# Second MLP in pairs of column chunks, with seven block products in 32 of its units

## The reference

```python
h2 = _rms_norm(x, norm2_g[l])
x = x + (jax.nn.silu(h2 @ w_gate[l]) * (h2 @ w_up[l])) @ w_down[l]
```

## Time and profile before

| | |
|---|---|
| median of 3 runs | 2490.76 us (2490.45 to 2491.49) |
| the profiled execution's own time | 2491.81 us |
| its span | 2490.1 us |
| PE busy | 2479.4 us in 11851 matmuls |
| DVE, ACT, POOL busy | 1379.7, 1120.4, 116.4 us |
| moved by DMA | 467.11 MB, mean 188 GB/s |

### The profile page before, as it was taken

The page is one execution under the profiler, slowest core; times in us unless marked ns, Lnnn a source line. Parts: engine busy times, 40 slices in busy tenths (PEclk is TensorE's granted clock), DMA queues, the critical chain, the costliest instruction groups (busy, mean ns, idle before and its releaser), DMA issues.

```text
span 2490.1 us, 27992 instructions
## 1 busy us (share of the span) xinstructions
PE 2479.4 (100%) x11851; PEld 2073.6 (83%) x11851; DVE 1379.7 (55%) x1130; ACT 1120.4 (45%) x1100; POOL 116.4 (5%) x95
## 2 busy tenths in 40 slices
PE   9999999999999999999999999999999999999999
PEld 7888888888888888888888888788888888888887
DVE  5775455454655555545555568876544444444444
ACT  5545533334444434334434458874533333333332
POOL 0410010010100000000000010000200000000000
PEclk9999999999999999999999999999999999999999
DMA  7555465656656555555555555444555655565554
GB/s 250 174 181 185 154 202 186 202 187 199 223 189 204 194 191 186 197 191 186 195 191 188 186 186 186 138 160 160 186 186 186 198 191 186 187 200 187 187 190 147
DMA packets 243306, 467.11 MB, mean 188 GB/s; under 512 B 11312, under 2 KB 23104, under 8 KB 242798
## 3 DMA queue, kind: packets, MB, share of 16 engines
q1 hardware_dynamic: 241630, 460.08, 56.8%
q10 hardware_dynamic: 1552, 5.25, 0.6%
HBM read 463.20 MB, written 2.10 MB: 187 GB/s over the span
## 4 chain that ended last, share of the span: by engine, by line
PE 97%; DVE 1%; ACT 1%; issue 0%; DMA 0%; POOL 0%; SPq 0%; DVEq 0%; ACTq 0%; POOLq 0%
PE acc L423 26%; PE acc L414 26%; PE acc L416 26%; PE acc L443 5%; PE acc L449 2%; PE tp L443 2%; PE sd L443 2%; PE sd L449 1%; PE tp L449 1%; PE tp L469 1%; PE sd L1377 1%; PE tp L1395 0%; DVE wlo L399 0%; PE sd L1386 0%; ACT whi L391 0%
## 5 line engine op out<-in xcount | busy, mean ns | idle before, releaser
L399 DVE TENSOR_TENSOR wlo<-raw,whi 128x2048 fp32r<-128x2048 f32 (+1 forms) x440 | 1014.0, 2306 | 955.7 <-ACT whi L391 955.0
L391 ACT ACTIVATE whi<-raw 128x2048 fp32r<-128x2048 f32 (+1 forms) x440 | 832.3, 1893 | 1068.7 <-PE acc L423 920.3
L414 PE MATMUL acc<-whi,opA_hi 128*128 128x512 f32 x1888 | 741.1, 393 | 0.0
L416 PE MATMUL acc<-whi,opA_lo 128*128 128x512 f32 x1888 | 735.4, 390 | 0.0
L423 PE MATMUL acc<-wlo,opA_hi 128*128 128x512 f32 x1888 | 469.2, 390 | 0.2 <-DVE wlo L399 0.2
L414 PE MATMUL acc<-whi,opB 128*128 128x512 f32 (+1 forms) x1088 | 422.3, 389 | 1.5 <-ACT whi L391 1.5
L416 PE MATMUL acc<-whi,opB 128*128 128x512 f32 (+1 forms) x1088 | 419.0, 386 | 0.0
L414 PEld LDWEIGHTS acc<-whi,opA_hi 128*128 128x128 f32 x1888 | 354.8, 188 | 73.9 <-issue 0.9
L416 PEld LDWEIGHTS acc<-whi,opA_lo 128*128 128x128 f32 x1888 | 354.8, 188 | 72.6
L423 PEld LDWEIGHTS acc<-wlo,opA_hi 128*128 128x128 f32 x1888 | 353.0, 188 | 73.4 <-DVE wlo L399 0.8
L423 PE MATMUL acc<-wlo,opB 128*128 128x512 f32 (+1 forms) x1088 | 266.4, 387 | 0.1
(11 more groups left out here) (307 smaller groups left out, 1286.8 us busy)
## 6 DMA issues: line engine op xcount, KB each, us to landing
raw<-in_w_in SPq DMA_DIRECT2D x114, 1024.0 KB, 5.5
raw<-in_w_mlp_up SPq DMA_DIRECT2D x64, 1024.0 KB, 5.5
raw<-in_w_mlp_down SPq DMA_DIRECT2D x64, 1024.0 KB, 5.0
raw<-in_w_gate SPq DMA_DIRECT2D x44, 1024.0 KB, 5.1
raw<-in_w_up SPq DMA_DIRECT2D x44, 1024.0 KB, 5.2
raw<-in_w_down SPq DMA_DIRECT2D x44, 1024.0 KB, 5.0
raw<-in_w_out SPq DMA_DIRECT2D x32, 1024.0 KB, 5.0
raw<-in_w_branch SPq DMA_DIRECT2D x16, 1024.0 KB, 5.0
```

The source lines that it names most:

```text
L391: eng.activation(whi[:, j % SPL, k, 0:cols], raw[:, j, k, 0:cols], ACT.Copy).then_inc(hi_split, share(k))
L399: eng.tensor_tensor(wlo[:, j % SPL, k, 0:cols], raw[:, j, k, 0:cols], whi[:, j % SPL, k, 0:cols].bitcast(F32), ALU.subtract).then_inc(lo_s ...
L414: eng.matmul(acc[:, pair, m, 0:cols], hi[:, kt + i, m * P:(m + 1) * P], whi[:, s, i, 0:cols], start=first and i == 0, stop=False)
L416: eng.matmul(acc[:, pair, m, 0:cols], lo[:, kt + i, m * P:(m + 1) * P], whi[:, s, i, 0:cols], start=False, stop=False)
```

## The change

A **pair** takes two runs in one: for a chunk c a gate pair does gate and up together, and a down pair does two neighbouring 512-column chunks of the output. A unit is now 2 k-tiles by 2 chunks (b = 0, 1), loaded by two DMAs of 512 KB, and all four banks `acc[:, b, m]` are in use by each pair. 17 pairs: in the parts of 3, 4 and 4 chunks, gate pairs of 8 units and two down pairs of 6, 8 and 8.

A plain unit has the same 24 matmuls. In a pair's first and last unit they go bank by bank (6 each, high then low), since the four banks are emptied and freed one by one (bank_done, bank_read, silu_in).

A **seven-unit** multiplies its 2 x 2 blocks of activations (m by k-tile) and 2 x 2 blocks of weights (k-tile by b) with seven products of sums in place of eight (Strassen's scheme in Winograd's form): 21 matmuls. Gate pairs have them at v = 3 and 5 (the first at 5 alone), down pairs at 3 and 5 (in part 0: the first at 3, the second at 1 and 3). It needs
- sums of the weight blocks: GpSimd, `weight_sums`, three instructions into t_sum, one buffer;
- seven blocks split high and low: `seven_high` on ACT (four copies, hi_split raised after the first two and after the last), `seven_low` on DVE (three instructions);
- sums of the activation blocks (a_hi, a_lo), made once for a part and place: `operand_sums` on DVE, a copy on ACT, `operand_low` on DVE one unit later. A_SUMS places them: in the first pair at v = 1 and 2, then at v = 1 of each part's last gate pair and of its first down pair.

The products go to four banks of their own (sd and tp) and to three of acc. At a pair's last unit `combine` joins them, after ACT has copied one to q_sum; `finish_first` and `finish` add them to the banks or to xres, ahead of and behind the low split of the next pair's first unit. t_sum lies at 160 KB of SBUF for 8 KB, a_full and a_sum at 164 and 166.

The diff, cut to its core:

```diff
+PAIR_UNITS = KT // 2
+GATE_SEVEN, DOWN_SEVEN = (3, 5), (3, 5)
...
+PAIRS = []
+unit, chunks2, seven2 = G_PAIR0 * UN, 0, 0
+for part, size in enumerate((CH2_FIRST, CH2_LOOP, CH2_LOOP)):
+    for c in range(size):
+        PAIRS.append(Pair(len(PAIRS), "gate", unit, PAIR_UNITS, GATE_SEVEN if PAIRS else GATE_SEVEN[1:], 0,
+                          GATE_SEVEN, (part, c), chunks2))
+        unit += PAIR_UNITS
+        chunks2 += 1
+    for n in range(2):
+        seven = DOWN_SEVEN if part else (1, 3) if n else (3,)
+        PAIRS.append(Pair(len(PAIRS), "down", unit, size * CT // 2, seven, 1, DOWN_SEVEN if part else (1, 3),
+                          (part, n), chunks2))
+        unit += size * CT // 2
+for p in PAIRS:
...
+A_SUMS = {(0, 1): (0, GATE_SEVEN[0], 0), (0, 2): (0, GATE_SEVEN[1], 1)}
+for q in PAIRS:
+    if q.kind == "gate" and PAIRS[q.n + 1].kind == "down":
+        A_SUMS[q.n, 1] = (1, PAIRS[q.n + 1].places[0], 0)
+        A_SUMS[q.n + 1, 1] = (1, PAIRS[q.n + 1].places[1], 1)
...
+    for p in PAIRS:
...
+        for v in range(p.units):
+            u = p.unit + v
+            sp.wait_ge(lo_split, (u - RAW + 1) * HV)
+            to = raw[:, u % RAW].rearrange("p (a b) c -> p a b c", a=2)
+            for b in range(2):
+                if p.kind == "gate":
+                    src = (w_gate2, w_up2)[b][:, 2 * v:2 * v + 2, chunk(first + n)]
+                else:
+                    src = w_dn2[:, first * CT + 2 * v:first * CT + 2 * v + 2, chunk(2 * n + b)]
+                sp.dma_start(to[:, :, b, :], src).then_inc(landed[u % RAW], 16)
...
+    def weight_sums(p, v):
+        u, n = p.unit + v, sevens_before(p, v)
+        w = raw[:, u % RAW]
+        pool.wait_ge(landed[u % RAW], loads_before(u // UN + 1) * 16)
+        if last_seven(p, v):
+            pool.wait_ge(lo_split, last_seven(p, v) * HV)
+        pool.wait_ge(a_low, sum(x < (p.n, v) for x in A_SUMS))
+        pool.tensor_tensor(t_sum[:, 0:2, :], w[:, 0:4:3, :], w[:, 1:2, :].to_broadcast([P, 2, NW]),
+                          ALU.add).then_inc(t_made, 1)
+        pool.wait_ge(t_made, 3 * n + 1)
+        pool.tensor_tensor(t_sum[:, 2, :], t_sum[:, 0, :], w[:, 3, :], ALU.add).then_inc(t_made, 1)
+        pool.wait_ge(t_made, 3 * n + 2)
+        pool.tensor_tensor(t_sum[:, 3, :], t_sum[:, 2, :], w[:, 2, :], ALU.add).then_inc(t_made, 1)
...
+    def seven_high(p, v):
+        u, n = p.unit + v, sevens_before(p, v)
+        act.wait_ge(landed[u % RAW], loads_before(u // UN + 1) * 16)
+        if last_seven(p, v):
+            act.wait_ge(units_used, last_seven(p, v))
+        act.activation(seven_hi[:, 0, :], raw[:, u % RAW, 0, :], ACT.Copy)
+        act.activation(seven_hi[:, 1:3, :], raw[:, u % RAW, 2:4, :], ACT.Copy).then_inc(hi_split, 1)
+        act.wait_ge(t_made, 3 * n + 1)
+        act.activation(seven_hi[:, 3:5, :], t_sum[:, 0:2, :], ACT.Copy)
+        act.wait_ge(t_made, 3 * n + 3)
+        act.activation(seven_hi[:, 5:7, :], t_sum[:, 2:4, :], ACT.Copy).then_inc(hi_split, 1)
...
+    for p in PAIRS:
+        for v in range(p.units):
+            if v in p.seven:
+                seven_high(p, v)
+            else:
+                hi_unit(act, (p.unit + v) // UN, (p.unit + v) % UN)
+            if p.n == 0 and v < UN:
+                side2(12 * UN + v)
+            if v == 0 and p.n and PAIRS[p.n - 1].kind == "gate":
+                silu_gates(PAIRS[p.n - 1])
+            if v == 2 and p.n and PAIRS[p.n - 1].kind == "gate":
+                turned_hi(act, T_HID2 + (p.turned - 1) * MT, opA_hi, PAIRS[p.n - 1].chunk[1] * CT)
+            if (p.n, v) in A_SUMS:
+                k, _, x = A_SUMS[p.n, v]
+                act.wait_ge(a_made, list(A_SUMS).index((p.n, v)) + 1)
+                act.activation(a_hi[k][:, x, :, :], a_sum[:, :, :], ACT.Copy).then_inc(a_high, 1)
...
+            if v == p.units - 1:
+                act.wait_ge(units_used, p.unit + p.seven[-1] + 1)
+                if p.n:
+                    last = PAIRS[p.n - 1]
+                    act.wait_ge(*((bank_read, 4 * last.n + 1) if last.kind == "gate" else (combined, last.combined + 4)))
+                act.activation(q_sum[:, :], sd[:, 0, :], ACT.Copy).then_inc(q_copied, 1)
...
+    def bank_free(p, b, m):
+        if p.n == 0:
+            pe.wait_ge(read_dve, readers_before(R_PAIR0 - 1 + b, "D") * MT)
+        elif PAIRS[p.n - 1].kind == "gate" and b == 0:
+            pe.wait_ge(silu_in, PAIRS[p.n - 1].gates * MT + m + 1)
+        else:
+            pe.wait_ge(bank_read, 4 * (p.n - 1) + 2 * b + m + 1)
...
+        banks = [(b, m) for b in range(2) for m in range(MT)]
+        if first or last:
+            for b, m in banks:
+                if first:
+                    bank_free(p, b, m)
+                for a in range(2):
+                    high(b, m, a)
+                pe.wait_ge(lo_split, (u + 1) * HV)
+                for a in range(2):
+                    mm = low(b, m, a)
+                if last and (b, m) != banks[-1]:
+                    mm.then_inc(bank_done, 1)
...
+        mm.then_inc(units_used, 1)
...
+    def seven_products(p, v, hi, lo):
+        u = p.unit + v
+        first, last, x = v == p.seven[0], v == p.seven[-1], p.places.index(v)
+        k1, k2, up, down = 2 * v, 2 * v + 1, slice(0, P), slice(P, T)
+        sums = lambda i: (a_hi[p.op][:, x, i, :], a_lo[p.op][:, x, i, :])
+        own = [(sd[:, 0, :], (hi[:, k1, up], lo[:, k1, up]), 0, True),
+               (acc[:, 0, 0, :], (hi[:, k2, up], lo[:, k2, up]), 1, False),
+               (acc[:, 1, 0, :], sums(0), 2, False)]
+        made = [(sd[:, 1, :], sums(1), 3, True), (tp[:, 1, :], sums(2), 4, True), (tp[:, 0, :], sums(3), 5, True),
+                (acc[:, 0, 1, :], (hi[:, k2, down], lo[:, k2, down]), 6, False)]
...
+        pe.wait_ge(a_low, sums_made(p, v))
+        for done, products in ((1, own), (2, made)):
+            pe.wait_ge(hi_split, u * HV + done)
+            for bank, (a_h, a_l), i, alone in products:
+                pe.matmul(bank, a_h, seven_hi[:, i, :], start=alone and first, stop=False)
+                pe.matmul(bank, a_l, seven_hi[:, i, :], start=False, stop=False)
+            pe.wait_ge(lo_split, u * HV + done)
+            for bank, (a_h, a_l), i, alone in products:
+                mm = pe.matmul(bank, a_h, seven_lo[:, i, :], start=False, stop=alone and last)
+        mm.then_inc(units_used, 1)
...
+    def seven_low(p, v):
+        u, n = p.unit + v, sevens_before(p, v)
+        w = raw[:, u % RAW]
+        if last_seven(p, v):
+            dve.wait_ge(units_used, last_seven(p, v))
+        dve.wait_ge(hi_split, u * HV + 1)
+        dve.tensor_tensor(seven_lo[:, 0, :], w[:, 0, :], seven_hi[:, 0, :].bitcast(F32), ALU.subtract)
+        dve.tensor_tensor(seven_lo[:, 1:3, :], w[:, 2:4, :], seven_hi[:, 1:3, :].bitcast(F32),
+                          ALU.subtract).then_inc(lo_split, 1)
+        dve.wait_ge(hi_split, u * HV + 2)
+        dve.wait_ge(t_made, 3 * n + 3)
+        dve.tensor_tensor(seven_lo[:, 3:7, :], t_sum[:, :, :], seven_hi[:, 3:7, :].bitcast(F32),
+                          ALU.subtract).then_inc(lo_split, 1)
...
+    def operand_sums(p, v):
+        op, unit, _ = A_SUMS[p.n, v]
+        n = list(A_SUMS).index((p.n, v))
+        hi, lo = ((opB_hi, opB_lo), (opA_hi, opA_lo))[op]
+        kt = slice(2 * unit, 2 * unit + 2)
...
+        if n:
+            dve.wait_ge(lo_split, last_seven(p, v) * HV)
+            dve.wait_ge(a_low, n)
+        own.done(dve.tensor_tensor(a_full[:, :, :], hi[:, kt, :].bitcast(F32), lo[:, kt, :].bitcast(F32), ALU.add))
+        a11, a21, a12, a22 = [a_full[:, r, m * P:(m + 1) * P] for r in range(2) for m in range(MT)]
+        own.mark(dve.tensor_tensor(a_sum[:, 1, :], a21, a22, ALU.subtract))
+        own.done(dve.tensor_tensor(a_sum[:, 2, :], a21, a11, ALU.subtract))
+        own.done(dve.tensor_tensor(a_sum[:, 3, :], a22, a_sum[:, 2, :], ALU.subtract))
+        dve.tensor_tensor(a_sum[:, 0, :], a12, a_sum[:, 3, :], ALU.subtract).then_inc(a_made, 1)
+    def operand_low(p, v):
...
+        dve.wait_ge(a_made, n + 1)
+        dve.wait_ge(a_high, n + 1)
+        dve.tensor_tensor(a_lo[op][:, x, :, :], a_sum[:, :, :], a_hi[op][:, x, :, :].bitcast(F32),
+                          ALU.subtract).then_inc(a_low, 1)
+    def combine(p):
+        dve.wait_ge(units_used, p.unit + p.seven[-1] + 1)
+        n = p.combined
+        dve.wait_ge(q_copied, p.n + 1)
+        if p.n:
+            dve.wait_ge(combined, n)
+            dve.wait_ge(bank_read, 4 * p.n)
+        dve.tensor_tensor(vw[:, 0, :], tp[:, 0, :], q_sum[:, :], ALU.subtract).then_inc(combined, 1)
+        dve.wait_ge(combined, n + 1)
+        dve.tensor_tensor(vw[:, 1, :], tp[:, 1, :], vw[:, 0, :], ALU.add).then_inc(combined, 1)
+        dve.wait_ge(combined, n + 2)
+        dve.tensor_tensor(yz[:, :, :], vw[:, :, :], sd[:, 1:2, :].to_broadcast([P, 2, NW]), ALU.add).then_inc(combined, 1)
+        if p.kind == "down":
```

(79 more changed lines are left out.)

213 lines of the change are left out of this document (80 added, 133 removed).

## The result

The changed kernel takes 2506.24 us (median of 5 runs, 2503.71 to 2508.58), the kernel before beside it on the same chip 2490.76 (5 runs, 2490.45 to 2491.78): a ratio of 1.0062, 95% interval 1.0047 to 1.0076, 15.5 us slower. The forecast was 2516.5, in a range of 2485 to 2530. The profiled execution took 2508.45 us, its span 2506.7; it lies 2.2 us above the median, with a mean granted clock of 0.997 over its span, where the other four have 0.998 or 0.999.

The account below looks back on a forecast made before the run. TensorE was taken to bound the kernel, working 2479.4 of 2490.1 us. The terms -21.8 + 30.0 + 15.3 + 2.2 = +25.7 us gave 2517.5, or 2516.5 for the median; range 2485 to 2530.

Parts of the forecast that it names:

- step A: Six pairs, seven-units at v = 3 and 5: weight sums wait for operand sums, so TensorE waits; +30.0 us.
- removed matmuls: Seven-units of the second MLP: 96 matmuls go, at 0.2267 us each; -21.8 us.
- step B: Five boundaries from a down pair to the next: combine and GpSimd's sum delay the low split; +15.3 us.
- step C: First pair: operand sums at v = 1 and 2 delay the high split of v = 3; +2.2 us.
- Longer sums: Rival on GpSimd's weight sums: strided and broadcast inputs lengthen them, 1 us more gives 2527.5 us; chance 0.14.
- At nothing: Items priced at zero: two loads per unit, silu behind VectorE's sum, the tail, TensorE's added waits on flags long set.
- The first rival: Operand split comes early enough, so step A costs 0; -13.3 us, 2477.5 us; chance 0.16.

Follow-up runs that it names:

- e3: Changed kernel, but GpSimd's sums for v = 3 wait until the low split of the pair's first unit is done: 2501.55 us.
- e4: Changed kernel with plain products in all units, neither operand sums nor combine; same pairs, loads, transposes and stores: 2489.73 us.
- e5: Changed kernel with operand sums in their own buffer and sums into xres behind the next low split, last pair's order kept: 2473.11 us.
- e9: As e5, but one operand's sums at v = 2 of the first pair, the other's at v = 1 of the second: 2471.82 us.
- e7: Kernel before the change, with idle VectorE work ahead of one low split at five places of the second MLP: 2513.3 us.

## Why the prediction came out as it did

The sign, the places and the two mechanisms were right; the size was not, 25.7 forecast and 18.4 in the stage. The step that failed is the size of step A, 30.0 forecast for 20.7 measured, and a term was missing: the half clock, 5.4.

| | forecast | measured |
|---|---|---|
| removed matmuls | -21.8 | -21.8 |
| step A | +30.0 | +20.7 |
| step B | +15.3 | +11.9 |
| step C | +2.2 | +1.9 |
| half clock | - | +5.4 |
| gaps not assigned | - | +0.3 |
| sum | +25.7 | +18.4 |

Of the 10.3 us by which the forecast of the median missed, 7.3 are this difference and 1.7 the earlier start of the stage; the rest is that the profiled execution after lies further above its median than the one before.

**Removed.** The count fell by 96, and the pairs without waits show that each is worth 0.2267 us.

**Step A.** What was mis-sized is VectorE's schedule between N and N + 14.15. I had packed it too loosely, and each piece came sooner: the low split of v = 1 began at N + 2.44, not 2.95, the high split of v = 2 at N + 7.1, not 7.9, `operand_low` ended 0.95 us sooner. The turns on the ports were as drawn: 3.41 for 1.23 us of the second `seven_lo` instruction, as in the earlier trace rows. The third sum was 1.15 us sooner, and the wait 1.5 instead of 2.7. At v = 5 it was 0.95 for 1.5, as it hangs on v = 3's low half; the low halves waited 0.38 for 0.55 to 0.6. An error of 1 us at one point of a chain is paid again at each unit that hangs on it: about 9 us in all. (The upper bound of this step, 87, is 85 by its own terms, 30 + 11 x 5.)

**Step B.** "GpSimd's first sum ... starts at about L + 4.4, ahead of the low split" came true twice in four times. All four races are decided by 0.09 to 0.24 us, less than a sum with terms taken to 0.1 us can foretell; the forecast should have priced two outcomes, not one. The boundary inside part 0 took 1.95 + 1.11 us for 3.3, the two where GpSimd was first 2.94 and 2.85 for 3.0, the other two 0.75 and 1.09, less than the 1.3 named as the lower bound; 1.2 more are the slower first matmuls and small gaps around these waits. That each race is worth 2 us of waiting, and the half clock that came with it, is what e3 shows. At the low splits the trace agrees with the rule that I had cited of the Trainium skill ("SBUF — State Buffer", "Who interferes with whom": an exclusive lock, issue order decides), in both directions: 4.46 for 2.28, and 4.43 for 2.39.

**Step C** took 1.63 + 0.16 + 0.12 = 1.9 us for 2.2.

**The missing term.** "So only matmuls that vanish give time, and every new wait of TensorE costs its full length" was too low a price for the long waits. At half clock behind them it is their length and then 1.4 to 3 us more. It went the other way than A's and B's errors, 5.4 against 12.7, so that the total was off by less than its parts; that it came near is in part luck.

**Longer sums** (the third rival) did not occur: where no split holds the ports the first takes 2.39 us and the third 1.28 (both in rows above), as in the earlier trace rows, with strided and broadcast inputs. What was added is waiting for the ports. Groups of GpSimd in the second MLP (busy, mean ns of one, then idle time before):

```profile
L944 POOL TENSOR_TENSOR t_sum<-raw 128x1024 f32<-128x1024 f32 x32 | 95.0, 2967 | 513.1 <-DVE ad_lo L2453 194.2 <-DMA raw<-in_w_up 145.3 <-issue 117.9
L947 POOL TENSOR_TENSOR t_sum<-t_sum,raw 128x512 f32<-128x512 f32 x32 | 57.8, 1807 | 2.5
L949 POOL TENSOR_TENSOR t_sum<-t_sum,raw 128x512 f32<-128x512 f32 x32 | 48.4, 1511 | 2.5
```

Of 513.1 us idle 194.2 end with `ad_lo`, the wait for the buffer; the row counts the idle time before the weights landed too.

**At nothing.** For the loads and the added waits e4 confirms it, to 0.01 us in the stage. It has neither ScalarE's new copies nor silu behind VectorE's sum; in the changed kernel TensorE waits for none of these except where A and C say so, and the tail took 4.1 us for 4.2.

**The first rival** (cover holds, 2477.5) was the right picture of what the change could have been: e5 and e9 are that case, without the boundary waits that it allowed for. It needed another buffer, and for the boundaries another order on VectorE, which the changed kernel doesn't have.

## What to carry to other kernels

Before helper work is given to an idle engine, look at what its buffer lies over: here two small tiles shared by address made GpSimd, with its input there, start over 14 us late, and that cost nearly as much as all the removed matmuls brought. Where two engines take turns on one pair of ports, put a wait that fixes who comes first, or move what nobody waits for behind what somebody does. And price a short wait of TensorE at its listed idle time plus 0.3 us, one of 3 us at nearly 2 us more, for slower matmuls behind it; the second price was not paid at one of e7's five waits in the profiled execution.
